# Taps of a convolution placed by unit length, a residual chain with three bank pairs and its transposes first, and a layer-norm root on 8 columns

## The reference

```
px = split(modulate(x) @ w_in)         # q, forget f/b, v, gate, conv a, conv b
ox = bidirectional gated recurrence(q, k, v, log f), 4 heads of 128
a  = rms(ox) * silu(gate)
u  = conv_a * sigmoid(conv_b)
y  = depthwise conv, width 31, over rows of 64 tokens, 512 channels
b  = silu(layer_norm(y))
x  = x + gate1 * rms(concat(a, b) @ w_out)
x  = x + gate2 * rms(swiglu(modulate(x)))
```

## Time and profile before

| | |
|---|---|
| median of 3 runs | 1555.27 us (1553.86 to 1555.57) |
| profiled execution | 1554.48 us |
| its span in the trace | 1552.7 us |
| PE busy | 1407.6 us, 91% |
| PE weight loads busy | 1168.9 us, 75% |
| DVE busy | 782.5 us, 50% |
| ACT busy | 370.8 us, 24% |
| POOL busy | 319.1 us, 21% |
| mean granted clock of PE | 0.941 |

### The profile page before, as it was taken

One profiled execution on the slowest core, in us unless ns is written; L12 is line 12 of the kernel. 1 busy time (PEld: TensorE's weight loads), 2 busy tenths in 40 slices (PEclk: granted clock), 3 DMA queues, 4 the chain that ended last, 5 costly groups with the idle time before them and its releaser, 6 DMA issues. The chain is left out here.

```text
span 1552.7 us, 17582 instructions
## 1 busy us (share of the span) xinstructions
PE 1407.6 (91%) x6709; PEld 1168.9 (75%) x6709; DVE 782.5 (50%) x1051; ACT 370.8 (24%) x533; POOL 319.1 (21%) x135
## 2 busy tenths in 40 slices
PE   6798999799989968796677899999999999999998
PEld 2587888688778855585556778888888888888876
DVE  1999786678578587816462131323313223232327
ACT  2511321222122215714231201121111111111112
POOL 1621111211011014402140412212222122221210
PEclk8699899899999979899788999999999999999999
DMA  9392100000010020003320201110111101111132
GB/s 370 133 328 79 41 28 28 28 27 14 27 41 27 14 95 1 1 12 126 93 81 13 69 27 55 55 55 28 53 54 54 53 28 54 54 54 38 43 136 109
DMA packets 94703, 101.93 MB, mean 66 GB/s; under 512 B 3118, under 2 KB 77091, under 8 KB 94658
## 3 DMA queue, kind: packets, MB, share of 16 engines
q1 hardware_dynamic: 94658, 101.32, 19.1%
HBM read 92.92 MB, written 8.39 MB: 65 GB/s over the span
## 5 line engine op out<-in xcount | busy, mean ns | idle before, releaser
L1223 POOL TENSOR_TENSOR slot<-slotraw,slot 128x1024 fp32r<-128x1024 f32 x66 | 158.7, 2427 | 533.1 <-ACT slot L1159 342.5
L560 PE MATMUL bank<-h2Ta,slot 128*128 128x512 f32 x1056 | 250.0, 396 | 18.8 <-POOL slot L1223 11.9
L560 PE MATMUL bank<-slot,mid 128*128 128x512 f32 x1056 | 244.7, 393 | 5.4 <-DVEq L1706 3.6
L560 PEld LDWEIGHTS bank<-h2Ta,slot 128*128 128x128 f32 x1056 | 202.2, 192 | 62.1 <-POOL slot L1223 12.6
L560 PEld LDWEIGHTS bank<-slot,mid 128*128 128x128 f32 x1056 | 200.3, 190 | 48.3 <-DVEq L1706 4.0
L560 PE MATMUL bank<-cathi,slot 128*128 128x512 f32 x704 | 221.7, 391 | 5.9 <-POOL catlo L1223 5.9
L560 PE MATMUL bank<-hT,ringb 128*128 128x512 f32 (+1 forms) x672 | 158.2, 394 | 14.7 <-POOL ringb L1223 14.7
L1405 DVE SCALAR_TENSOR_TENSOR cat<-conv_u,taps,cat 128x784 f32 (+29 forms) x120 | 159.8, 1332 | 12.4 <-DVE cat L1405 3.8
L560 PEld LDWEIGHTS bank<-cathi,slot 128*128 128x128 f32 x704 | 133.1, 189 | 33.9 <-issue 6.1
L560 PEld LDWEIGHTS bank<-hT,ringb 128*128 128x128 f32 x672 | 125.4, 199 | 39.4 <-issue 10.3
L1670 DVE TENSOR_TENSOR mid<-bank,sgm 128x512 f32<-128x512 f32 x44 | 30.4, 692 | 234.4 <-ACT sgm L1174 234.4
(11 more groups left out here) (167 smaller groups left out, 1524.3 us busy)
## 6 DMA issues: line engine op xcount, KB each, us to landing
mraw<-in_w_mod SPq DMA_DIRECT2D x48, 512.0 KB, 7.3
slotraw<-in_ffn_w_gate SPq DMA_DIRECT2D x22, 512.0 KB, 3.8
slotraw<-in_ffn_w_up SPq DMA_DIRECT2D x22, 512.0 KB, 4.8
slotraw<-in_ffn_w_down SPq DMA_DIRECT2D x22, 512.0 KB, 3.9
ringinb<-in_w_in SPq DMA_DIRECT2D x12, 512.0 KB, 3.6
xst<-in_x SPq DMA_DIRECT2D x8, 512.0 KB, 13.8
ringina<-in_w_in SPq DMA_DIRECT2D x8, 512.0 KB, 4.6
ringinc<-in_w_in SPq DMA_DIRECT2D x8, 512.0 KB, 4.7
```

Of the source, the lines that this page charges most:

```text
L560: return pe.matmul(o, l, r, start=start, stop=stop, skip_group_check=True)
L1223: return pool.tensor_tensor(lo, full, hi.bitcast(F32), ALU.subtract)
```

## The change

There are three edits.

1. `TAPS_AFTER`: the number of taps in units 8 to 19 goes from 2, 2, 2, 2, 2, 2, 2, 2, 2, 3, 3, 2 to 3, 2, 4, 4, 3, 3, 3, 3, 0, 1, 0, 0. The same 30 taps are made in the same order.
2. The layer norm's variance becomes a product with one column of ones for each token block (32 products of one column), the root (`ln_roots`) and the reciprocal (`rstds`) work on 128x8 in the new tile `lss`, and `rb`, two entries of `TAIL`, spreads the 8 columns over 128x512 by products with the identity. `normed` reads the bank. DVE centres both halves at unit 1. The entries of `TAIL` and ACT's and POOL's lists around them are put in a new order; among them, ACT makes the hi parts of three inputs and three weight blocks before level 0.
3. `mix(t)` takes the pair `(2t + n) % 6`, waits for the sum of t-3 instead of t-2, and `turn2(t-4)` stands ahead of `mix(t)`.

```diff
-TAPS_AFTER = [0, 0, 0, 0, 1, 1, 1, 1, 2, 2, 2, 2, 2, 2, 2, 2, 2, 3, 3, 2]
+TAPS_AFTER = [0, 0, 0, 0, 1, 1, 1, 1, 3, 2, 4, 4, 3, 3, 3, 3, 0, 1, 0, 0]
...
-TAIL = [("sum", 0), ("sum", 1), ("var", 0), ("part", 4, 0), ("part", 4, 1), ("part", 5, 0), ("var", 1),
-        ("part", 5, 1), ("part", 6, 0), ("part", 6, 1), ("part", 7, 0), ("part", 7, 1)]
+TAIL = [("sum", 0), ("sum", 1), ("part", 4, 0), ("part", 4, 1), ("part", 5, 0), ("var",), ("part", 5, 1),
+        ("rb", 0), ("rb", 1), ("part", 6, 0), ("part", 6, 1), ("part", 7, 0), ("part", 7, 1)]
...
-                    for j in range(4):
-                        pe.wait_ge(ln_square, u[1] * 4 + j + 1)
-                        ins = mm(b[:], ones[:], sig_t[:, 4 + j, u[1] * BANK:(u[1] + 1) * BANK], j == 0, j == 3)
+                    pe.wait_ge(ln_square, 8)
+                    for ch in range(XT):
+                        for j in range(4):
+                            ins = mm(b[:, ch:ch + 1], sig_t[:, 4 + j, ch * P:(ch + 1) * P], ones[:, 0:1], j == 0, j == 3)
+                elif u[0] == "rb":
+                    pe.wait_ge(ln_rstd, 1)
+                    for cc in range(4):
+                        ins = mm(b[:, cc * P:(cc + 1) * P], view(lss, XT + u[1] * 4 + cc, [(0, P)]), ident[:], True, True)
...
-                if t >= 2:
-                    pe.wait_ge(mix_sum, 2 * t - 2)
+                if t >= 3:
+                    pe.wait_ge(mix_sum, 2 * t - 4)
...
-                        ins = mix_step(bank[(2 * t + n) % 4], t, n, k, k == ks[0], k == ks[-1])
+                        ins = mix_step(bank[(2 * t + n) % 6], t, n, k, k == ks[0], k == ks[-1])
...
             for t in range(XT):
-                mix(t)
                 if t >= 4:
                     turn2(t - 4)
+                mix(t)
...
-            cat_parts(0)
+            for k in range(3):
+                cat_parts(k)
+            for i in range(3):
+                wo_hi(i)
             rec_act(0)
-            wo_hi(0)
-            cat_parts(1)
-            cat_parts(2)
             rec_act(1)
-            wo_hi(1)
-            wo_hi(2)
             squares(0)
+            squares(1)
             rec_act(2)
-            squares(1)
-            ln_roots(0)
-            takes(("part", 4, 0))
+            takes(("part", 4, 0), ("part", 4, 1))
             rec_act(3)
+            takes(("part", 5, 0))
+            ln_roots()
...
-                dve.reciprocal(r, r).then_inc(ln_rstd, 1)
+                dve.reciprocal(lss[:, 1, :], lss[:, 0, :]).then_inc(ln_rstd, 1)
...
-                if u == 1 or u == 2:
-                    centre(u - 1)
-                elif u == 4 or u == 6:
-                    rstds(u // 2 - 2)
-                    normed(u // 2 - 2)
-                elif u == 5 or u == 7:
-                    swish(u // 2 - 2)
+                if u == 1:
+                    centre(0)
+                    centre(1)
+                elif u == 3:
+                    rstds()
+                elif u == 4 or u == 5:
+                    normed(u - 4)
+                elif u == 6 or u == 7:
+                    swish(u - 6)
```

More of the change, by code:

```diff
@@ L118 @@
 EARLY = [0, 1, 2]
-TAIL = [("sum", 0), ("sum", 1), ("var", 0), ("part", 4, 0), ("part", 4, 1), ("part", 5, 0), ("var", 1),
-        ("part", 5, 1), ("part", 6, 0), ("part", 6, 1), ("part", 7, 0), ("part", 7, 1)]
+TAIL = [("sum", 0), ("sum", 1), ("part", 4, 0), ("part", 4, 1), ("part", 5, 0), ("var",), ("part", 5, 1),
+        ("rb", 0), ("rb", 1), ("part", 6, 0), ("part", 6, 1), ("part", 7, 0), ("part", 7, 1)]
 TAIL += [("full", t, n) for t in range(4) for n in range(2)] + [("gate", 0), ("gate", 1)]
-TAIL_BY = ["dve" if u[0] == "sum" else "act" for u in TAIL]
-TAIL_AT = [0, 0, 2, 2, 3, 3, 4, 4, 5, 5, 6, 6, 7, 8, 9, 9, 10, 10, 11, 11, 12, 12]
+TAIL_BY = ["dve" if u[0] in ("sum", "rb") else "act" for u in TAIL]
+TAIL_AT = [0, 0, 2, 2, 3, 3, 4, 4, 4, 5, 5, 6, 6, 7, 7, 8, 8, 9, 10, 10, 11, 12, 12]
 TRING = 3
@@ L199, in kernel_program @@
         hss = sb("hss", [P, 2, XT])
+        lss = sb("lss", [P, 2, XT])
         align(512)
@@ L790, in mix @@
                     pe.wait_ge(use_dve, (HEADS + 1) * N_UDVE)
-                else:
+                elif t == 0:
                     pe.wait_ge(tail_act, TAIL_BY.count("act"))
+                    pe.wait_ge(tail_dve, TAIL_BY.count("dve"))
                     pe.wait_ge(o_lo, KT)
@@ L1044, in squares, with ln_roots @@
                     act.activation(sig_t[:, 4 + j, sl], cat[:, 4 + j, sl], ACT.Square).then_inc(ln_square, 1)
-            def ln_roots(hf):
-                i = TAIL.index(("var", hf))
+            def ln_roots():
+                i = TAIL.index(("var",))
                 act.wait_ge(tail_full, i + 1)
-                act.activation(rstd[:, hf * BANK:(hf + 1) * BANK], bank[i % TRING][:], ACT.Sqrt, bias=eps[:],
+                act.activation(lss[:, 0, :], bank[i % TRING][:, 0:XT], ACT.Sqrt, bias=eps[:],
                                scale=1.0 / BANK).then_inc(tail_act, 1)
@@ L1087, in _ @@
             act.wait_ge(use_dve, HEADS * N_UDVE)
-            cat_parts(0)
+            for k in range(3):
+                cat_parts(k)
+            for i in range(3):
+                wo_hi(i)
             rec_act(0)
-            wo_hi(0)
-            cat_parts(1)
-            cat_parts(2)
             rec_act(1)
-            wo_hi(1)
-            wo_hi(2)
             squares(0)
+            squares(1)
             rec_act(2)
-            squares(1)
-            ln_roots(0)
-            takes(("part", 4, 0))
+            takes(("part", 4, 0), ("part", 4, 1))
             rec_act(3)
+            takes(("part", 5, 0))
+            ln_roots()
             wo_hi(3)
-            takes(("part", 4, 1), ("part", 5, 0))
             rec_act(4)
+            takes(("part", 5, 1))
+            wo_hi(4)
             swish_sig(0)
-            ln_roots(1)
-            takes(("part", 5, 1))
             rec_act(5)
-            wo_hi(4)
-            wo_hi(5)
             act.wait_ge(q_ready, (HEADS - 1) * NK + 2)
             takes(("part", 6, 0), ("part", 6, 1))
+            wo_hi(5)
+            swish_sig(1)
             rec_act(6)
@@ L1115, in _ @@
             ln_parts(0)
-            swish_sig(1)
             takes(("part", 7, 0), ("part", 7, 1))
@@ L1119, in _ @@
             ln_parts(1)
+            takes(("full", 0, 0), ("full", 0, 1))
             rec_act(8)
-            takes(("full", 0, 0), ("full", 0, 1))
+            takes(("full", 1, 0), ("full", 1, 1))
             rec_act(9)
-            takes(("full", 1, 0), ("full", 1, 1))
+            takes(("full", 2, 0))
             rec_act(10)
-            takes(("full", 2, 0), ("full", 2, 1))
+            takes(("full", 2, 1), ("full", 3, 0))
             rec_act(11)
-            takes(("full", 3, 0), ("full", 3, 1))
+            takes(("full", 3, 1))
             rec_act(12)
@@ L1614, in mix_add @@
                     dve.wait_ge(mix_full, 2 * t + n + 1)
-                    dve.tensor_tensor(part[t][:, sl], bank[(2 * t + n) % 4][:], part[t][:, sl], ALU.add).then_inc(mix_sum, 1)
+                    dve.tensor_tensor(part[t][:, sl], bank[(2 * t + n) % 6][:], part[t][:, sl], ALU.add).then_inc(mix_sum, 1)
                 dve.wait_ge(mix_sum, 2 * t + 2)
```

13 lines of the change are left out of this document (7 added, 6 removed).

## The result

The changed kernel takes 1495.03 us (median of 4 runs, 1494.26 to 1497.1); the kernel before took 1555.01 (4 runs) beside it. The ratio is 0.9617, 95% interval 0.9601 to 0.9634: faster by 60.0 us, where 64 were forecast. The profiled execution took 1495.62 us.

A forecast was written before the change was run, and what follows sets the result against it. PE was bound by waits for K queued behind DVE's taps, tail holes (ACT's wide root), and turn-taking with DVE in the chain. 17.2 + 16.3 + 30.5 = 64.0 off 1554.48 gave 1490.5, forecast 1491 us; range 1484 to 1499 (52%).

The forecast's parts named there:

- parts 1 and 3: Taps moved earlier, ending PE's waits for K at two borders, 17.2 us; residual chain paced by DVE alone, 30.5 us.
- three signs of being wrong: PE waits for S at "o"; PE idle above 10 us before level 3; PE waits for DVE's add or row load.
- part 2: Third border, tail and layer norm: 21.4 us credits, 2.1 and 5 debits, 2 more credited; 16.3 us gained, between 7 and 23.
- K 11.5 us earlier: Head loop: eight taps of 1.44 us moved from ahead of K; waits and low clock at two borders go, 17.2 us.
- The price of the fourth tap, 0: Unit 10's fourth tap starts 0.1 to 0.2 us before POOL's split, costing 0; if POOL is first, "o" 2.0 late per head.
- the rival: Crowded scan: POOL precedes the fourth tap; "o" 2.0 us late in three heads, up to 2.6 more each; 1497 to 1505; 20%.
- The third border, 10.5 + 2.7: Level-0 products start right behind the last V: the 10.53 us wait goes, and 2.7 us of low clock.
- The layer norm, 5.6 + 2.6 + 2 against 2.1 + 5, a gain of 3.1: Tail: root wait 5.6, low clock 2.6, freed DVE and ACT 2; against narrow products and spreading 2.1, tail's front 5.
- the 10.2 of credit: Layer-norm credits: 5.6 us root wait, 2.6 low clock after it, 2 for DVE and ACT freed of reciprocal and table loads.
- The chain, 29.5 to the first feed-forward product: Residual chain: DVE's 8.15 us per row block sets the pace; first feed-forward product at 756.7 instead of 786.18, 29.5 us gained.

The follow-up runs named there:

- e1: The kernel before with the new TAPS_AFTER table alone (old tail, old chain): 1527.20 us, ratio 0.9825.
- e4: The changed kernel with one tap moved from unit 10 to unit 12: 1491.43 us, ratio 0.9601.
- e9: The kernel before with e4's tap table and both chain edits, keeping the old layer-norm tail: 1488.69 us, ratio 0.9584.
- e13: e4 with e10's wait, e12's columns, and 64 columns too for the 8 products per head summing squares of the output: 1485.28 us, ratio 0.9549.
- e12: e4 with its 64 variance records given 64 equal columns instead of one: 1487.90 us, ratio 0.9571.
- e10: e4 with POOL's low-part copies of wo blocks 0 to 2 waiting until DVE has written the last head's two level-1 queries: 1487.98 us, ratio 0.9584.
- e3: The changed kernel with the old tap table and old residual chain, leaving only the new layer norm and tail order: 1560.37 us, ratio 1.0043.

## Why the prediction was right, and where it was off

The time fell into the range and 4 us from the number, and the mechanisms of parts 1 and 3 hold. Of the three signs of being wrong that I had named, one came: PE waits for S at "o". PE's idle time before level 3 is 0.48 + 4.57 + 1.11 = 6.2 us, not above 10, and in the chain PE waits for no add and no row load. That part 2 came near its number is partly luck: the 13.1 us are the third border, and the gain of the layer norm, 3.1 in the sum, was not there. By steps:

- **K 11.5 us earlier.** Right. The waits at all three borders and the low clock with them are gone, 17.2 us at the first two.
- **The price of the fourth tap, 0.** Wrong by its sign: a lead of 0.1 to 0.2 us for the tap was in truth one of 0.03 for POOL. "o" waits 1.70 us in three heads, 5.1 in sum, where I had named 2.0 each for this case. It was in the sum with the wrong value and among the rivals with the right one, at 20%; the rival's further 2.6 us a head for the clock didn't come. From the first scan round it took 502.38 - 495.42 = 6.96 us to the tap and 6.93 to POOL's block. For POOL I had 6.94, for the tap 6.8 to 6.9: the round and the gap behind it were 2.81 long, not 2.7. An instant worked out from rows to some 0.4 us can't decide a race of 0.1, and the step should have carried half of the price. The rule of the Trainium skill cited there ("SBUF — State Buffer", section "SBUF: two separate sides") is that the operation that starts first keeps the shared lock for its whole length. Both traces agree: the tap behind a POOL block took 3.11 us before and 3.40 after.
- **The third border, 10.5 + 2.7.** Right: 3.84 us with a wait of 0.48. e1 has it with the taps alone.
- **The layer norm, 5.6 + 2.6 + 2 against 2.1 + 5, a gain of 3.1.** Wrong. The wait for the root did go, and yet the tail is longer by 0.35 us (the changed kernel against e1) or by 0.5 (e4 against e9, up to `hss`). The debits were larger than mine. The stopped query costs 4.57 us, near my 5, but 1.5 of it stand in the old tail too. The narrow products took 9.38 instead of 7.4, and 1.8 more came behind them, both by the clock; the spreading took 1.95. Against the old tail that is 3.0 + 2.2 + 1.95 + 1.8 = 8.9, an estimate from these rows, and would leave 1.3 of the 10.2 of credit as gain. So about 1.8 us of the credit was missing too. Which of its three terms is not shown; each was time won in the midst of a stretch in which PE, DVE and ACT hand work to each other, and was booked at its full length. I had read the 1.84 us of 16 such records as their price for any number. It is their price as long as the clock is full.
- **The chain, 29.5 to the first feed-forward product.** Right at 30.2. DVE sets the pace at 8.16 us, where 8.15 was worked out; PE needs 7.7 for a row block, where I had 8.0. I had priced the two edits as one, but each alone gives most of it: the transposes ahead 30.7 us, the bank pairs 27.4, both 31.3.

In the spans 64.0 - 58.9 = 5.1 us are missing: 4.2 in the loop (the 5.1 of the readout, less 0.9 that the bodies gained elsewhere) and 3.2 in the tail, less 1.0 more at the start and 1.2 more in the chain and behind it.

## What to carry to other kernels

Test the parts of a change alone: here one of three was worth nothing with the others and cost 6.5 us without them, and a sum of 60 us hid it. Its faults, once found, could be mended (e13). Where two engines exclude each other, look for places where their operations start within some tenths of a microsecond, and move one by a whole operation: one tap moved from unit 10 to unit 12 was worth 3.6 us by the medians and 6.4 in the traces. If a reduction on TensorE has only one column on its moving side, look at the granted clock of its stretch and of the one behind it, and try more columns; they were free here.

## What the runs showed of the hardware

- With PE counted as busy for the whole of each stretch, the granted clock fell from 1.00 to 0.50 within a stream of 64 one-column records (9.38 to 9.72 us). With 64 columns in the same records it stayed at 1.00 (7.25 us). At full clock a record with 64 columns starts every 3 / 29 = 0.10 us (e12), and so does one with one column (e10, 29 from 577 to 580); at the low level one with one column starts every 3 / 15 = 0.20.
- A start 0.03 us ahead was enough for POOL to hold the tap back until its block was over (3.40 instead of 1.23 us). POOL's blocks back to back don't shut DVE out, they alternate: in e3 blocks of POOL begin at 569.26 and 572.36 and take 3.13 and 3.10 us, and taps begin at 570.33 and 573.40 and take 2.93 and 2.90. Free ones take 2.4 and 1.0 to 1.3. Twelve taps went from 17.23 to 22.81 us in this way.
